# Conformer and attention layer on one core: six places for centring, sums of output weights every 2.6 groups, and a re-ordered last row block

## What is computed

```python
z = jnp.einsum("bsd,de->bse", h, w_in) + b_in          # 512 x 2048 times 2048 x 14352
glu_val, glu_gate, gate_c, q, k, v, f_logit, gate_a = _split_columns(z)
y_conv = _conformer_conv(glu_val, glu_gate, w_dw, b_dw, g_conv_norm, b_conv_norm)  # 31 taps, then a layer norm over 2048 channels
y_conv = y_conv * jax.nn.silu(gate_c)
y_attn = _forgetting_attention(q, k, v, f_logit) * jax.nn.silu(gate_a)             # 16 heads of 128
y = jnp.concatenate([y_conv, y_attn], axis=-1)
sub = jnp.einsum("bse,ed->bsd", y, w_out) + b_out      # 512 x 4096 times 4096 x 2048
h = _layer_norm(DN_ALPHA * h + sub, g_post, b_post)
```

## Time and profile before

| | |
|---|---|
| runs | 1602.7, 1600.45, 1598.1 us (median 1600.45) |
| profiled execution | 1602.69 us; its span, from first to last instruction, 1600.9 us |
| PE busy | 1557.6 us (97%), PE weight loads 1491.3 |
| DVE, ACT, POOL busy | 1443.0, 839.4, 274.8 us |
| DMA | 367.33 MB, 229 GB/s; HBM read 286.73 MB, written 87.06 MB |
| issues to landing | `w_in` loads 8.1 us (224), `raw<-raw` 6.1 (112), POOL's sums of output weights 9.7 (64) |

### The profile page before, as it was taken

How to read it: one execution, slowest core, us unless ns; L and a number is a source line. 1 busy time by engine, 2 the same in 40 slices (tenths; PEclk the granted TensorE clock), 3 DMA queues, 4 the chain that set the end, 5 groups by cost and what they waited for, 6 DMA issues and landing times.

```text
span 1600.9 us, 29447 instructions
## 1 busy us (share of the span) xinstructions
PE 1557.6 (97%) x11574; PEld 1491.3 (93%) x11574; DVE 1443.0 (90%) x1952; ACT 839.4 (52%) x1224; POOL 274.8 (17%) x295
## 2 busy tenths in 40 slices
PE   7999999999999999999999999999998899999997
PEld 6989999999999999999999999999888888888885
DVE  7669999999999999999999999999967689996787
ACT  5565454554545545455454454554454476744462
POOL 1101112122021121211212212121223200000000
PEclk9999999999999999999999999999999999999998
DMA  8488888999989999899998999998998989887875
GB/s 225 112 199 188 225 203 211 237 210 241 234 204 234 210 249 227 206 238 233 230 221 213 238 232 225 223 222 218 209 276 236 269 296 347 301 232 248 258 213 182
DMA packets 316761, 367.33 MB, mean 229 GB/s; under 512 B 14593, under 2 KB 254369, under 8 KB 315313
## 3 DMA queue, kind: packets, MB, share of 16 engines
q1 hardware_dynamic: 284880, 260.45, 53.1%
q0 software_dynamic: 27360, 100.68, 34.5%
q10 hardware_dynamic: 4384, 4.33, 0.8%
HBM read 286.73 MB, written 87.06 MB: 233 GB/s over the span
## 4 chain that ended last, share of the span: by engine, by line
PE 79%; DVE 9%; DMA 5%; issue 4%; ACT 1%; SPq 1%; POOL 0%; DVEq 0%; ACTq 0%; POOLq 0%
PE ps L1056 26%; PE ps L1057 26%; PE ps L1058 26%; DMA cin<-conv_rows_dram 3%; DVE whl L1308 3%; DVE c_tiles L1409 2%; PE ps L1173 1%; DMA raw<-raw 1%; DVE raw L1327 1%; DMA f_raw<-in_w_in_dram 1%; DMA conv_rows_dram<-c_tiles 1%; DVE raw L1319 1%; SPq L402 1%; DVE xl L1347 0%; ACT whl L781 0%
## 5 line engine op out<-in xcount | busy, mean ns | idle before, releaser
L1056 PE MATMUL ps<-xh,whl 128*128 128x256 f32 x3136 | 897.4, 286 | 22.2 <-DVE whl L1308 10.4
L1057 PE MATMUL ps<-xl,whl 128*128 128x256 f32 x3136 | 889.2, 284 | 0.0
L1058 PE MATMUL ps<-xh,whl 128*128 128x256 f32 x3136 | 889.1, 284 | 0.0
L781 ACT ACTIVATE whl<-raw 128x1024 fp32r<-128x1024 f32 x392 | 415.2, 1062 | 552.7 <-PE ps L1058 441.8
L1056 PEld LDWEIGHTS ps<-xh,whl 128*128 128x128 f32 x3136 | 601.2, 192 | 27.2 <-issue 13.8
L1057 PEld LDWEIGHTS ps<-xl,whl 128*128 128x128 f32 x3136 | 601.6, 192 | 0.5 <-issue 0.5
L1058 PEld LDWEIGHTS ps<-xh,whl 128*128 128x128 f32 x3136 | 601.3, 192 | 0.0
L1308 DVE TENSOR_TENSOR whl<-raw,whl 128x1024 fp32r<-128x1024 f32 x392 | 482.5, 1231 | 61.4 <-ACT whl L781 61.3
L1409 DVE SCALAR_TENSOR_TENSOR c_tiles<-ps,taps,c_tiles 128x511 f32<-128x511 f32 (+14 forms) x480 | 350.6, 730 | 6.8
L630 POOL DMA_DIRECT2D raw<-raw x56 | 49.9, 891 | 483.4 <-DMA raw<-in_w_in_dram 427.3
L1311 DVE TENSOR_TENSOR whl<-raw,whl 128x1024 fp32r<-128x1024 f32 x80 | 97.8, 1223 | 32.4 <-ACT whl L757 32.2
(11 more groups left out here) (185 smaller groups left out, 1552.6 us busy)
## 6 DMA issues: line engine op xcount, KB each, us to landing
raw<-in_w_in_dram SPq DMA_DIRECT2D x224, 512.0 KB, 8.1
raw<-raw POOLq DMA_DIRECT2D x112, 512.0 KB, 6.1
out_sums_dram<-in_w_out_dram POOLq DMA_DIRECT2D x64, 512.0 KB, 9.7
raw<-out_sums_dram SPq DMA_DIRECT2D x64, 512.0 KB, 5.1
raw<-in_w_out_dram SPq DMA_DIRECT2D x48, 512.0 KB, 5.2
out_sums_dram<-in_w_out_dram SPq DMA_DIRECT2D x32, 512.0 KB, 9.4
out_sums_dram<-out_sums_dram SPq DMA_DIRECT2D x32, 512.0 KB, 9.6
x<-in_x_dram SPq DMA_DIRECT2D x8, 512.0 KB, 8.1
```

Source lines behind the costliest of these rows:

```text
L781: nc.scalar.activation(w_high(n), source(n), ACT.Copy).then_inc(high_done, 1)
L1056: nc.tensor.matmul(o, ah, bh, start=start, stop=False, skip_group_check=True)
L1057: nc.tensor.matmul(o, ah, bl, start=False, stop=False, skip_group_check=True)
L1058: return nc.tensor.matmul(o, al, bh, start=False, stop=True, skip_group_check=True)
```

## The change

Four parts. (1) Centring has six places: the four of `cin`, and the tensors `rstd` and `csum`, which are not in use then (`csum` from the mean's matmul on). A load waits for the square and the store of six tiles back, not four. (2) ACT's squares move one slot later, to slots 3, 5, 6 and slot 1 of the next group. (3) T1 and T3 of tile k are copied in group 3 + 13k // 5, T2 three groups after, T4 six after, and each copy's addition is in the same group (T3's one later); the last is in group 48, where it was 55. Two loads of stage 2's first operands move later in SP's order. (4) At the end, block t = 0 takes the way of blocks 2 and 3 (ACT scales, POOL adds `b_post` by DMA), block t = 1 goes in quarters of 512 columns, and each product is followed by its statistics. Some semaphores are merged (`ns1_done`, `s2_done`, `s3_done` into one, `mean_done` and `var_done` into one, `fw_done` into `fw_high`); this moves no instruction.

```diff
+CIN = 6
...
+SUMS_AT = tuple(3 + 13 * k // 5 for k in range(HEADS))
...
+        def cin_slot(j):
+            n = j % CIN
+            return cin[:, n, :] if n < 4 else (rstd, csum)[n - 4][:, :]
...
             def load_cin(j):
-                if j >= 4:
-                    sp.wait_ge(sq_done, j - 3)
-                    sp.wait_ge(cent_stored[j % 4], 16 * (j // 4))
-                sp.dma_start(cin[:, j % 4, :], conv_dram[j, :, :]).then_inc(cin_loaded[j % 4], 16)
+                if j >= CIN:
+                    sp.wait_ge(sq_done, j - CIN + 1)
+                    sp.wait_ge(cent_stored[j % CIN], 16 * (j // CIN))
+                elif j == CIN - 1:
+                    sp.wait_ge(mean_var_done, 1)
+                sp.dma_start(cin_slot(j), conv_dram[j, :, :]).then_inc(cin_loaded[j % CIN], 16)
...
-                if g % 3 == 0 and 0 <= g // 3 - 2 < HEADS:
-                    k = g // 3 - 2
-                    sp.wait_ge(t_added[T1], 16 * (k + 1))
-                    if k:
-                        sp.wait_ge(t2_copied, 16 * k)
-                    copy_sum(T2, k, t_dram[T1, k, :, :], t2_copied)
-                if g % 3 == 1 and 0 <= g // 3 - 3 < HEADS:
-                    k = g // 3 - 3
-                    sp.wait_ge(t_added[T2], 16 * (k + 1))
-                    if k:
-                        sp.wait_ge(t4_copied, 16 * k)
-                    copy_sum(T4, k, t_dram[T2, k, :, :], t4_copied)
-                if g % 3 == 0 and 0 <= g // 3 - 1 < HEADS:
-                    k = g // 3 - 1
-                    if k:
-                        sp.wait_ge(t13_copied, 32 * k)
-                    copy_sum(T1, k, w_out[D + P * k:D + P * (k + 1), 0:1024], t13_copied)
-                    copy_sum(T3, k, w_out[D + P * k:D + P * (k + 1), 1024:], t13_copied)
+                for k in range(HEADS):
+                    if g == SUMS_AT[k] + 6:
+                        sp.wait_ge(t_added[T2], 16 * (k + 1))
+                        if k:
+                            sp.wait_ge(t4_copied, 16 * k)
+                        copy_sum(T4, k, t_dram[T2, k, :, :], t4_copied)
+                    if g == SUMS_AT[k] + 3:
+                        sp.wait_ge(t_added[T1], 16 * (k + 1))
+                        if k:
+                            sp.wait_ge(t2_copied, 16 * k)
+                        copy_sum(T2, k, t_dram[T1, k, :, :], t2_copied)
+                    if g == SUMS_AT[k]:
+                        if k:
+                            sp.wait_ge(t13_copied, 32 * k)
+                        copy_sum(T1, k, w_out[D + P * k:D + P * (k + 1), 0:1024], t13_copied)
+                        copy_sum(T3, k, w_out[D + P * k:D + P * (k + 1), 1024:], t13_copied)
...
             load_a(0, 0)
-            load_a(0, 1)
             sp.wait_ge(low_done, at(g, 2) + 1)
             sp.wait_ge(t4_in[g % 2], parity(g))
             load_out(3)
-            sp.wait_ge(unit_done, at(g, 2) + 1)
-            load_a(0, 2)
-            for n in range(4):
-                sp.wait_ge(cent_stored[n], 64)
-            sp.wait_ge(unit_done, at(g, 3) + 1)
-            load_c(0)
+            for n in range(CIN):
+                sp.wait_ge(cent_stored[n], 48 if n < 4 else 32)
+            load_a(0, 1)
             sp.wait_ge(low_done, at(g, 4) + 1)
             load_out(4)
-            load_a(0, 3)
+            load_c(0)
             for par in range(2):
                 sp.wait_ge(z1_stored[par], 48)
                 sp.wait_ge(z2_stored[par], 48)
             for u in range(OUT_RING, OUT_UNITS):
                 sp.wait_ge(low_done, out_n(u - OUT_RING) + 1)
                 load_out(u)
+                if u in (6, 10):
+                    load_a(0, 2 if u == 6 else 3)
...
-            for t in (2, 3):
+            for e, t in enumerate((2, 3, 0)):
                 for h in range(2):
                     c = slice(1024 * h, 1024 * (h + 1))
-                    sp.wait_ge(bpost_added, 16 * (2 * (t - 2) + h + 1))
+                    sp.wait_ge(bpost_added, 16 * (2 * e + h + 1))
                     sp.dma_start(out[0, P * t:P * (t + 1), c], res[t][:, c]).then_inc(stored, 16)
-            for t in range(2):
-                for h in range(2):
-                    c = slice(1024 * h, 1024 * (h + 1))
-                    sp.wait_ge(row_done, 2 * t + h + 1)
-                    sp.dma_start(out[0, P * t:P * (t + 1), c], res[t][:, c]).then_inc(stored, 16)
-            sp.wait_ge(stored, 32 * NT)
+            for n in range(4):
+                c = slice(SEQ * n, SEQ * (n + 1))
+                sp.wait_ge(row_done, n + 1)
+                sp.dma_start(out[0, P:2 * P, c], res[1][:, c]).then_inc(stored, 16)
+            sp.wait_ge(stored, 160)
...
-                    add_sum(T2, k, w_out[row:row + P, 1024:])
+                    if g == SUMS_AT[k] + 6:
+                        add_sum(T4, k, w_out[row:row + P, 0:1024])
+                    if g == SUMS_AT[k] + 3:
+                        add_sum(T2, k, w_out[row:row + P, 1024:])
+                    if g == SUMS_AT[k] + 1:
+                        add_sum(T3, k, w_out[row:row + P, 1024:])
+                    if g == SUMS_AT[k]:
+                        add_sum(T1, k, w_out[D + P * k:D + P * (k + 1), 1024:])
...
+            for e, t in enumerate((2, 3, 0)):
                 for h in range(2):
                     c = slice(1024 * h, 1024 * (h + 1))
-                    if (t, h) != (2, 0):
-                        pool.wait_ge(bpost_added, 16 * (2 * (t - 2) + h))
-                    pool.wait_ge(rows_scaled, 2 * (t - 2) + h + 1)
+                    if e + h:
+                        pool.wait_ge(bpost_added, 16 * (2 * e + h))
+                    pool.wait_ge(rows_scaled, 2 * e + h + 1)
...
-                    if HEAD_GROUPS + 3 <= g < HEAD_GROUPS + 7 and s in (2, 4, 5):
-                        square(4 * (g - HEAD_GROUPS - 3) + (2, 4, 5).index(s))
-                    if HEAD_GROUPS + 3 < g <= HEAD_GROUPS + 7 and s == 0:
+                    if HEAD_GROUPS + 3 <= g < HEAD_GROUPS + 7 and s in (3, 5, 6):
+                        square(4 * (g - HEAD_GROUPS - 3) + (3, 5, 6).index(s))
+                    if HEAD_GROUPS + 3 < g <= HEAD_GROUPS + 7 and s == 1:
                         square(4 * (g - HEAD_GROUPS - 4) + 3)
 
...
+            def scale_rows(e):
+                act.wait_ge(fin_vec, INVERSE_AT[e] + 4)
                 for h in range(2):
-                    act.wait_ge(scaled_done, 2 * (t - 2) + h + 1)
-                    r = res[t][:, 1024 * h:1024 * (h + 1)]
-                    nc.scalar.activation(r, r, ACT.Copy, scale=rs[:, t - 2:t - 1]).then_inc(rows_scaled, 1)
...
+            def last_product(t, g):
+                dve.wait_ge(end_done, 2 * t + g + 1)
+                add_product(2, t, g, t, 0, ALU.add)
+                dve.wait_ge(c11_read, 2 * t + g + 1)
+                vec.bn_stats(stats[:, t, g, :], result(t, 0, g)).then_inc(stats_done, 1)
+
+            def scale_quarter(e, n):
+                t, c = (2, 3, 0, 1)[e], slice(SEQ * n, SEQ * (n + 1))
+                vec.scalar_tensor_tensor(out=res[t][:, c], in0=res[t][:, c], scalar=mv[:, 2 * e:2 * e + 1], in1=gpost_b[:, c],
+                                         op0=ALU.subtract, op1=ALU.mult).then_inc(scaled_done, 1)
+
+            last_product(0, 0)
+            last_product(0, 1)
+            dve.wait_ge(stats_done, 14)
+            moments(2)
+            scale_half(2, 0)
+            inverse(2)
+            scale_half(2, 1)
+            last_product(1, 0)
+            last_product(1, 1)
+            dve.wait_ge(stats_done, 16)
+            moments(3)
+            c, base = slice(3, 4), INVERSE_AT[3]
+            scale_quarter(3, 0)
+            scale_quarter(3, 1)
+            dve.wait_ge(fin_act, 4)
+            vec.reciprocal(rs[:, c], std[:, c]).then_inc(fin_vec, 1)
+            scale_quarter(3, 2)
+            dve.wait_ge(fin_vec, base + 1)
+            vec.scalar_tensor_tensor(out=newton[:, c], in0=rs[:, c], scalar=var_eps[:, c], in1=rs[:, c],
+                                     op0=ALU.mult, op1=ALU.mult).then_inc(fin_vec, 1)
+            scale_quarter(3, 3)
+            dve.wait_ge(fin_vec, base + 2)
+            vec.tensor_scalar(newton[:, c], newton[:, c], -0.5, 1.5, ALU.mult, ALU.add).then_inc(fin_vec, 1)
+            dve.wait_ge(fin_vec, base + 3)
+            vec.tensor_tensor(rs[:, c], rs[:, c], newton[:, c], ALU.mult).then_inc(fin_vec, 1)
+            dve.wait_ge(fin_vec, base + 4)
+            dve.wait_ge(scaled_done, 10)
+            for n in range(4):
+                c = slice(SEQ * n, SEQ * (n + 1))
+                vec.scalar_tensor_tensor(out=res[1][:, c], in0=res[1][:, c], scalar=rs[:, 3:4], in1=bpost_b[:, c],
+                                         op0=ALU.mult, op1=ALU.add).then_inc(row_done, 1)
 
 
```

97 lines of the change are left out of this document (33 added, 64 removed).

## The result

| | before | after |
|---|---|---|
| runs in one comparison | 1598.1 to 1603.8 us (4), median 1601.58 | 1638.1 to 1647.2 us (4), median 1641.61 |
| ratio | | 1.0258 (95% interval 1.0236 to 1.0280) |
| span of the profiled execution | 1600.9 us | 1638.4 us |
| groups 9 to 48 of stage 1 | 877.7 us | 918.2 us |
| groups 51 to 55 | 122.5 us | 117.0 us |

The forecast was 1598 us and the range ended at 1609. The profiled spans differ by 37.5 us: +40.5 in groups 9 to 48, -5.5 in groups 51 to 55, +2.9 at the end, and -0.4 at the start. In what follows a group begins with the first matmul of its slot 0, and "stage 1's middle" is groups 9 to 48.

A forecast was written before the change was run, and what follows sets the result against it. PE was taken as the bound, with 20.5 us excess in groups 51 to 55 and a 12 us end. Terms -6.3 + 1.5 - 4 + 4 + 2.3 = -2.5 us, from 1600.45 to 1598 us; range 1586 to 1609.

The forecast's parts named there:

- Part 3: Stage 1: earlier sums fit on average, but third additions in a row make PE wait in three groups: +4 us.
- rival A: Sums fit at no cost, the end is not longer, the clock stays up: 1587 us, chance 0.28.
- The free time: Groups of stage 1: 1.0 us more DMA work in a group, against 1.1 us that are free.
- What a delay costs: A third addition delays the last `w_in` block and `sum_3` by 2.9 us; PE waits 1 to 2 us.
- The count: Three additions in a row, where two was the most, in eight groups; waits expected in three of them.
- Rival B: DMA engines bound groups 9 to 42: three additions ahead of `sum_3`, 1.9 us in each of eight; 1610 us, chance 0.14.
- Part 1: Groups 51 to 55: tiles land sooner as the sums are gone; PE's 6.8 us for low parts become 0.5: -6.3 us.
- Part 2: Groups 52 to 55: later squares delay `sum_3`; PE's 6.5 us of waits for `p5` become 8: +1.5 us.
- rival C: Each `sum_3` of groups 52 to 55 a whole slot later, +7 us, clock still falls: 1604.5 us, chance 0.11.
- Clock and rest: Groups 51 to 55: with fewer, shorter waits, the excess other than waits falls from 7.2 to 3.2 us: -4 us.
- Part 4: The end: block 0's two `b_post` DMAs, 5.3 us each, hold back block 1's stores: +2.3 us.
- The weighed rule: By the skill's turns between queues loads keep half the engines, some +2 us; the trace was followed instead, +4.

The follow-up runs named there:

- Kernel 12: The kernel before with POOL's additions for the sums at most 1, 2, 1, 2 from group to group, oldest ready sum first: 1643.8 us, ratio 1.0276.
- kernel 8: The kernel before with T2's addition alone moved into T1's group, so additions 2, 2, 0 in three groups: 1661.8 us, ratio 1.0353.
- kernel 10: The kernel before with T3's and T4's additions one group later, so 1, 0, 3 in three groups: 1626.3 us, ratio 1.0141.
- kernel 6: The kernel before with T3's and T2's additions moved into T1's group, three in a row, no copy moved: 1662.8 us, ratio 1.0365.
- kernel 5: The kernel before with T4's copy one group earlier, four copies in a row, no addition moved: 1600.1 us, ratio 0.9981.
- kernel 2: The kernel before with only the changed timing of the sums: 1631.1 us, ratio 1.0178.
- kernel 13: The kernel before with the last sums (T2 of tile 15, T4 of tiles 14 and 15) formed in stage 2: 1598.8 us, ratio 0.9965.
- kernel 14: As kernel 13, with six places for centring besides: 1596.3 us, ratio 0.9960 to the kernel before.
- kernel 16: The kernel after with only the squares put back to their old slots: 1638.2 us, ratio 1.0220 to the kernel before.
- kernel 1: The kernel after with the sums' timing put back to that of before: 1606.2 us, ratio 1.0029 to the kernel before.
- kernel 3: The kernel after with sums started in group 3 + 3k, additions 3, 1, 0 in three groups: 1651.4 us, ratio 1.0313 to the kernel before.
- kernel 15: As kernel 14, with the squares one slot later: 1607.8 us, ratio 1.0024 to the kernel before.
- kernel 9: The kernel before with every copy and addition of the sums one group earlier, additions 2, 1, 1: 1602.4 us, ratio 0.9997.
- kernel 11: The kernel before with faster sums, at most 1, 2, 2 additions in three groups, oldest ready sum first: 1632.8 us, ratio 1.0195.
- kernel 17: As Kernel 12, with six places for centring: 1630.8 us, ratio 1.0183 to the kernel before.

## Why the prediction was wrong

**Part 3, the term that failed: the sums earlier.** "It fits, barely, on average" and "+4 us", bound +15; measured +40.5. The sum had two slips besides, which change nothing: ten transfers leave groups 49 to 55, not nine (six of them groups 51 to 55, not five), and rival A with a quarter of the forecast is 0.38. Three steps of the term were wrong.
- *The free time.* 1.1 us a group was read from the DMA share of 0.95. Kernel 12 adds no more than 0.17 additions to a group and loses 41.9 us. A share of 0.95 averaged over 300 us, with loads that must land by a deadline in every group, was no reserve.
- *What a delay costs.* The first link was right: one addition more puts `sum_3` off by its own 2.9 us, 3.1 and 2.9 us in the two groups shown. But I let the delay end there, in a wait of 1 to 2 us for `p5`. The blocks that SP loads beside it then meet the next burst and are held until its first addition has landed, so ACT waits 8.9 us for a `w_in` block, not for `sum_3`.
- *The count.* "Three in a row" named eight groups; two in a row do it as well (kernel 8), and three in a row elsewhere do a third of it (kernel 10 against kernel 6). Nor did PE's longer busy time after waits stand in this term: 16.8 of the 40.5 us, up to 12 of them clock.

Rival B had the right side and the right resource, but the same mechanism and price, and so ended at 1610; it named waits for blocks of `w_in` besides, but gave them no price. "Copies are hidden" was right (kernel 5).

**Part 1, six places.** The wait for low parts fell from 6.8 to 0, the forecast was -6.3: right in size, but the reason given, that the sums are gone, is only half of it. With them gone and old squares, 1.0, 3.4, 3.9 and 1.3 us remain (kernels 2, 13, 14, 16). With the sums still there and late squares it is 1.8 and 0 (kernels 1 and 3). So either brings most of it, and what brings it to 0 is part 2, which the prediction had only as a cost. That the places have a share is not shown (13 against 14, 2 against 16).

**Part 2, late squares.** +1.5 us was the second mis-sized term. The waits for `p5` are 9.1 us, as "6 to 10" said, but against kernel 16's 3.5 us without the move, and three groups stay at 0.93. What the move costs is not settled: in groups 51 to 55 8.3 us (after against 16) and 2.4 us (14 against 15), in the medians 3.4 us, within the noise, and 11.5 us, of which the slow addition on POOL may be a part. All four are over +1.5, and rival C's +7 lies among them.

**Clock and rest.** -4 us was forecast; PE's busy time fell by 1.3 (108.6 to 107.3 us). The sum 117.0 missed the stated 110 to 115 by about the clock's part, and both comparisons have the clock lower with late squares (three groups at 0.93 in the kernel after, none under 1.00 in kernel 16; 0.87, 0.93, 0.93 in kernel 15, one group at 0.94 in kernel 14).

**Part 4, the end.** +2.3 us forecast, +2.9 measured, here and in kernel 1. The second `b_post` DMA took 5.2 us where 5.3 was assumed, and it, not DVE's quarters, ends last, as said.

**The weighed rule.** I had taken the Trainium skill's turns between queues ("DMA: Bandwidth & Descriptors", Queues, rings and completion order) to mean that SP's loads keep half of the engines. The half doesn't follow from it. In the view of 346 to 352 us POOL's queue had 316 packets and SP's 203, so both were served, but one of POOL's took 0.991 x 96 / 316 = 0.30 us (16 engines for 6 us) and one of SP's 0.087 x 96 / 203 = 0.04 us. If turns were equal at these lengths, SP would have some 12% of the time, an estimate; it had 9%. So the trace doesn't speak against the rule as I had written, only against the half that I had drawn from it. Whether the packets that the profile counts are what the turns go by, no run here shows.

## What to carry to other kernels

When transfers are moved into a stage that never waits, ask for its tightest deadline, not its mean DMA share: look in the waits of the *other* engines for loads that are just caught in time, as the 4.8 us here. A late load that falls behind the next burst of another queue can be held for most of it (here 20.4 us to landing), so count what runs in any two or three neighbouring periods. And wherever PE is made to wait, add the longer busy time that comes with it, some of it clock: 0.7 us for each microsecond of idling in the kernel after, 0.5 in kernel 8. And one traced execution is one sample: look at where it lies among the kernel's runs before an edit is given the credit for a few us.

## What was not expected of the hardware

- While two accumulating DMAs of 512 KB from DRAM were moving on POOL's queue, SP's queue, with shorter packets, had 8 to 9% of the engines' time: 99.1 to 8.7% and 102.3 to 8.1% in the two views above. With one of them left, it had 46.0% beside 54.6%. A 512 KB load beside two of them took 19.8 and 20.4 us, where 3.8 us was the least in the middle of stage 1.
- PE's busy time grew by 16.8 us beside 23.6 us of idling in the kernel after, and by 22.3 beside 43.6 in kernel 8. Stretches at a granted clock of 0.50 explain at most 12.3 of the 16.8; kernel 9 has 4.3 us of it at 1.00.
- One and the same addition on POOL took 2.2 us in 14 of the profiled executions and 6.2 in six, and PE waited 4.0 us for it; why stays open.
- Some kernels with such a loss scatter more: four runs of kernel 2 span 17.5 us and four of kernel 11 span 23.5 us, where 29 of the kernel before span 14. Others don't: four of kernel 17 span 3 us. Why one burst catches a load and the next, alike in the order, doesn't, stays open; so does whether longer packets for `w_in` would end the starving, which wasn't tried.
